# Expert weights in tiles of 4 MB, a ring of 4 slots in place of 8, and two half tiles loaded while the branch products run

## Chip, cores and metric

One core of one Trainium2 chip. The metric is the device time of one execution in microseconds (us), lower is better.

## What is computed

One layer on 256 tokens of width 1024, in float32: a mixer (three attention branches, gates, output projection) and then a mixture of 32 experts, of which each token uses 4. The part that the change touches is the second:

```python
logits = (xt @ w_router + b_router)
top_v, top_e = lax.top_k(logits, TOP_K)          # 4 of 32 experts
wts = softmax(top_v)
# for each block of tokens of one expert e:
hdn = xblk @ w_mlp1[e] + b_mlp1[e]               # 1024 -> 2048
x_glu = minimum(hdn[:, ::2], 7.0)
x_lin = clip(hdn[:, 1::2], -7.0, 7.0)
act = x_glu * sigmoid(1.702 * x_glu) * (x_lin + 1.0)
y = act @ w_mlp2[e] + b_mlp2[e]                  # 1024 -> 1024
# weighted with wts and added to the token's row of x
```

w_mlp1 is 8 MB per expert (units of 2^20 bytes), w_mlp2 4 MB. The whole of both is read once, 402.65 MB (units of 10^6 bytes).

## The kernel before

**Stages.** The mixer runs first (to about 280 us). Its weights come in 40 units of 1 MB (`UNITS`), four in flight in the `raw` tiles (`MIX_RING`). ScalarE and VectorE split each unit in a high and a low part (`mix_high`, `mix_low`), TensorE multiplies. The last ten units are the branch projections (`br_moba0`, `br_ret0`, `br_mem0`, `br_moba1`, `br_ret1`, `br_mem1`) and the output projection (`out0`, `out1`). Then come the routing and the experts.

**Experts.** An item is one expert with up to 64 token slots. The first 30 items are written out, the rest are a loop on a register; with these inputs there are 32 items, one per expert. Of item j TensorE does, in this order and by a program written out by hand: the up products of j (`up`, L1456, four units u of 2 MB of w_mlp1), the gather of the tokens of j + 1 (L1431), the down products of j - 1 (`down`, L1462, two units v of 2 MB of w_mlp2), the transposes of the scatter matrix (L1477), of the next tokens (L1438) and of the activations of j (`act_transposes`, L1483, four of 128 x 128), the biases of j + 1 (L1444, L1446) and the scatter of j - 1 (L1492). Each product has two column halves: 64 slots by 512 columns go to PSUM partitions 0 to 63 and 64 to 127. In item 3 the late part of the routing and the bias of w_mlp2 (`b2`, L1422) stand between the gather and the down products.

**The last item** is written apart: after its up products come the down products of the item before, with `act_transposes` between their two halves, then its own down products, whose second 2 MB come in pieces of 1, 0.5 and 0.5 MB.

**The ring.** 16 MB of SBUF hold eight slots of 2 MB, 16 KB per partition in one contiguous piece of HBM (2 rows of w_mlp1 or 4 rows of w_mlp2). SyncE issues all loads in the order of `LOADS`: the four up units of item 0, then for each j the four up units of j and the two down units of j - 1. A load into a slot waits until TensorE has used what was in it (`up_used`, `down_used`, L511 and L514). Most slots lie over tiles of the mixer, so each of the first eight loads waits for its own part of the mixer (`mixer_left`):

```python
if slot <= 1:
    sp.wait_ge(unit_used, UNITS_DONE[GI["out0"] - 1])
    sp.wait_ge(silu_done, 2)
elif slot == 2:
    sp.wait_ge(y_done, 4)
elif slot == 3:
    sp.wait_ge(unit_used, N_MIX - 2)
```

**Other queues.** GpSimd issues small loads, among them that of `b_mlp2` (`b2s`, L577), which lies in a tile of the moba branch. ScalarE and VectorE each follow their own hand-written order.

Of the kernel before, what the change touches and what calls it, by code (L numbers as in the profile page):

```python
# [16 lines left out]
F32R = mybir.dt.float32r  # L17
# [3 lines left out]
ACT = mybir.ActivationFunctionType  # L21
AX = mybir.AxisListType

P = 128
# [53 lines left out]
USE = {load: n // SLOTS_N for n, load in enumerate(LOADS)}  # L78
LAST_DOWN = [(len(LOADS) + v) % SLOTS_N for v in range(W2U)]
assert not set(LAST_DOWN) & {SLOT[load] for load in LOADS[-IU:]}  # L80

# [123 lines left out]
def build(nc, a, out):  # L205
    ctx = ExitStack()
    with ctx:
# [10 lines left out]
        raw_pair = [sb(f"raw{i}", [P, 4096]) for i in range(MIX_RING // 2)]  # L218
        raw = [raw_pair[i // 2][:, 2048 * (i % 2):2048 * (i % 2) + 2048] for i in range(MIX_RING)]
        first = ExitStack()  # L220
        mix_hi = [sb(f"mix_hi{i}", [P, 2048], F32R, scope=first) for i in range(MIX_HL)]
        first.close()
        hi_pair = sb("hi_raw", [P, 2 * 2048])
# [44 lines left out]
        rt = sb("rt", [NE, 96])  # L268
        selw = sb("selw", [NE, 2, MAX_ITEMS])
        tabT = sb("tabT", [NE, 2, S])  # L270
        PG = sb("PG", [P, 2, TT, MAX_ITEMS])
        posi, gi = PG[:, 0, :, :], PG[:, 1, :, :]
        posm, G = posi[:, :, 0:NE], gi[:, :, 0:NE]
        bsel = sb("bsel", [64, MAX_ITEMS])
        items = sb("items", [1, MAX_ITEMS + 2], I32)

        mix = ExitStack()
# [14 lines left out]
        mix.close()  # L292

# [11 lines left out]
        b2s = o["moba"][0:NE, :, :].rearrange("p t n -> p (t n)")  # L305
        b1raw = PTs[0:64, :]

        merge_pair = [sb(f"merge_raw{i}", [P, 4096]) for i in range(2)]
        first = ExitStack()
        sb("branch_values", [P, 2048], scope=first)  # L310
        mix_hi.append(sb(f"mix_hi{MIX_HL}", [P, 2048], F32R, scope=first))
        first.close()
        value_pair = sb("value_raw", [P, 4096])
# [4 lines left out]
        gate_pair = sb("gate_raw", [P, 4096])  # L318
        b1s = sb("b1s", [P, FF2], F32R)
        prob_pair = sb("prob_raw", [P, 4096])  # L320
# [4 lines left out]
        ends = sb("b2_and_alibi", [P, 2048 + 1536 - 128 - 3 * 256])  # L325
# [4 lines left out]
        ring = merge_pair + [gate_pair, raw_pair[0], value_pair, raw_pair[1], hi_pair, prob_pair]  # L330
# [12 lines left out]
        ring_in = [sem(f"ring_in{i}") for i in range(SLOTS_N)]  # L343
        x_half = [sem(f"x_half{t}") for t in range(TT)]
# [43 lines left out]
        last_part = [sem(f"last_part{i}") for i in range(2)]  # L388
# [32 lines left out]
        def weight_tile(kind, j, u):  # L421

            if isinstance(j, int):
                load = (kind, j, u)
                return ring[SLOT[load]], ring_in[SLOT[load]], 16 * (USE[load] + 1)
            load = (kind, LOOPED if kind == "up" else LOOPED - 1, u)
            return ring[SLOT[load]], ring_in[SLOT[load]], 16 * j + 16 * (USE[load] + 1 - load[1])

        def last_down_tile(v):
            n = len(LOADS) + v  # L430
            return ring[LAST_DOWN[v]], ring_in[LAST_DOWN[v]], 16 * (n // SLOTS_N + 1)

# [23 lines left out]
        def _(sp):  # L456
            for m, (g, hk) in enumerate(UNITS):
# [20 lines left out]
                if m == 5:  # L478
                    sp.dma_start(memT, a["memT"]).then_inc(memT_in, 16)

            w1, w2 = a["w_mlp1"][0], a["w_mlp2"][0]

            def mixer_left(slot):

                if slot <= 1:
                    sp.wait_ge(unit_used, UNITS_DONE[GI["out0"] - 1])
                    sp.wait_ge(silu_done, 2)
                elif slot == 2:
                    sp.wait_ge(y_done, 4)
                elif slot == 3:  # L490
# [1119 lines left out]
```

## Time and profile before

| | |
|---|---|
| median of 3 runs | 1210.91 us (1210.24 to 1213.89) |
| the profiled execution | 1211.36 us |
| its span, first to last instruction | 1209.5 us |
| mean granted TensorE clock | 0.996 |
| PE busy | 1151.7 us (95%) |
| DVE, ACT, POOL busy | 410.5, 225.6, 8.7 us |
| HBM read | 453.11 MB, 375 GB/s over the span |
| expert loads | 191 of 2 MB, one of 1 MB, two of 0.5 MB |

The page calls TensorE's matmuls PE and its weight loads PEld; DVE is VectorE, ACT ScalarE, POOL GpSimd, SP SyncE and SPq its queue of DMA issues. A plain f32 product is recorded as two MATMULs, a transpose as one. "DMA share" is the mean busy share of the 16 DMA engines; it can read slightly over 1. "us to landing" counts from the issue of a DMA to its completion. Times of rows are from the start of the span.

### The profile page before, as it was taken

Reading aid. Unit: us, or ns where it says so; the run is one execution under the profiler, and the core shown is the slowest. Engines: PE = TensorE matmul, PEld = TensorE weight load, DVE = VectorE, ACT = ScalarE, POOL = GpSimd, SP = SyncE. Lnnn points to the kernel's source line nnn. Section 1 sums busy time; section 2 is a strip of 40 time slices with the busy share of each in tenths; the row PEclk is TensorE's granted clock in tenths of the full one; section 3 lists DMA queues with packets and bytes.
Section 4 is the critical chain, followed back from the end, with each engine's and each line's share of the span. In section 5 each row is a group of like instructions: output and inputs, shape, how many; then the busy total and the mean of one; then the engine's idle time right before and its main releaser. Section 6 shows DMA issues by size and latency. Waiting matters only on the chain.

```text
span 1209.5 us, 13242 instructions
## 1 busy us (share of the span) xinstructions
PE 1151.7 (95%) x5401; PEld 536.6 (44%) x5401; DVE 410.5 (34%) x677; ACT 225.6 (19%) x344; POOL 8.7 (1%) x17
## 2 busy tenths in 40 slices
PE   8999999999999999999999999998999999899997
PEld 5888888874333333333433333333333333333332
DVE  4865656864222222222222222222222222222221
ACT  3544447441000000010100000000000000000001
POOL 0100000000000000000000000000000000000000
PEclk9999999999998999999999999999999999999999
DMA  9755454599999999999999999999999999999995
GB/s 352 255 181 169 157 171 157 183 374 429 427 426 423 413 427 429 426 430 424 430 427 429 427 428 428 427 428 429 427 429 427 427 428 430 426 429 426 429 428 237
DMA packets 52322, 454.93 MB, mean 376 GB/s; under 512 B 4368, under 2 KB 4400, under 8 KB 27504
## 3 DMA queue, kind: packets, MB, share of 16 engines
q1 hardware_dynamic: 50816, 449.69, 89.8%
q0 software_dynamic: 784, 2.38, 0.5%
q10 hardware_dynamic: 672, 2.10, 0.5%
q8 instruction: 43, 0.70, 0.2%
q14 instruction: 7, 0.06, 0.0%
HBM read 453.11 MB, written 1.05 MB: 375 GB/s over the span
## 4 chain that ended last, share of the span: by engine, by line
PE 58%; DMA 40%; DVE 1%; issue 1%; ACT 0%; SPq 0%; DVEq 0%; ACTq 0%
PE PS L1456 19%; DMA merge_raw<-in_w_mlp 14%; DMA prob_raw<-in_w_mlp 14%; DMA raw<-in_w_mlp 12%; PE PS L1462 9%; PE PS L1273 6%; PE PS L1275 5%; PE PS L1274 5%; PE PS L1492 3%; PE PS L1431 2%; PE PS L1290 1%; PE PS L1269 1%; PE PS L1438 1%; PE PS L1344 1%; PE PS L1444 1%
## 5 line engine op out<-in xcount | busy, mean ns | idle before, releaser
L1456 PE MATMUL PS<-raw,XG 128*64 128x512 f32 x544 | 123.0, 594 | 11.2 <-DMA raw<-in_w_mlp 11.2
L1185 DVE TENSOR_SCALAR hT<-PS 128x512 f32<-128x512 f32 x32 | 22.1, 692 | 317.7 <-PE PS L1456 317.7
L779 ACT ACTIVATE hT<-hT 128x512 f32<-128x512 f32 x31 | 19.5, 630 | 553.0 <-DVE hT L1185 553.0
L1456 PE MATMUL PS<-merge_raw,XG 128*64 128x512 f32 x480 | 107.5, 596 | 6.2 <-DMA merge_raw<-in_w_mlp 5.9
L857 DVE TENSOR_TENSOR rest<-raw,mix_hi 128x2048 fp32r<-128x2048 f32 x38 | 87.0, 2291 | 55.2 <-ACT mix_hi L631 55.2
L1116 DVE COPY XG<-PS 128x512 f32<-128x512 f32 x32 | 22.1, 692 | 229.0 <-PE PS L1438 229.0
L1123 DVE TENSOR_TENSOR X<-X,PS 128x512 f32<-128x512 f32 x120 | 74.4, 682 | 53.1 <-PE PS L1492 53.1
L1273 PE MATMUL PS<-mix_hi,hTh 128*128 128x512 f32 x224 | 89.8, 401 | 0.0
L1275 PE MATMUL PS<-mix_hi,hTl 128*128 128x512 f32 x224 | 88.2, 394 | 0.0
L1274 PE MATMUL PS<-rest,hTh 128*128 128x512 f32 x224 | 88.1, 393 | 0.0
L631 ACT ACTIVATE mix_hi<-raw 128x2048 fp32r<-128x2048 f32 x38 | 72.6, 1913 | 42.9 <-PE PS L1275 39.9
L1456 PEld LDWEIGHTS PS<-raw,XG 128*64 128x64 f32 x544 | 38.2, 137 | 91.8 <-issue 72.7
L1456 PEld LDWEIGHTS PS<-merge_raw,XG 128*64 128x64 f32 x480 | 32.8, 137 | 77.7 <-issue 62.3
L1456 PE MATMUL PS<-gate_raw,XG 128*64 128x512 f32 x272 | 61.9, 597 | 2.1 <-DMA gate_raw<-in_w_mlp 2.1
L1462 PE MATMUL PS<-merge_raw,AT 128*64 128x512 f32 x256 | 57.4, 594 | 4.9 <-DMA merge_raw<-in_w_mlp 4.9
L1456 PE MATMUL PS<-value_raw,XG 128*64 128x512 f32 x272 | 62.0, 597 | 0.1
L765 ACT ACTIVATE Y<-PS 128x512 f32<-128x512 f32 x31 | 18.6, 599 | 225.4 <-PE PS L1462 225.4
L1431 PE MATMUL PS<-hx,SG 128*64 128x512 f32 x256 | 60.4, 593 | 0.0
L1456 PE MATMUL PS<-prob_raw,XG 128*64 128x512 f32 x240 | 54.3, 594 | 6.2 <-DMA prob_raw<-in_w_mlp 6.2
L1492 PE MATMUL PS<-Y,ST 64*128 64x512 f32 x240 | 59.6, 615 | 0.0
L1462 PE MATMUL PS<-raw,AT 128*64 128x512 f32 x224 | 50.9, 596 | 8.9 <-DMA raw<-in_w_mlp 8.9
L1456 PE MATMUL PS<-hi_raw,XG 128*64 128x512 f32 x240 | 54.6, 597 | 0.0
(272 smaller groups left out, 1246.8 us busy)
## 6 DMA issues: line engine op xcount, KB each, us to landing
raw<-in_w_mlp SPq DMA_DIRECT2D x48, 2048.0 KB, 34.1
merge_raw<-in_w_mlp SPq DMA_DIRECT2D x47, 2048.0 KB, 33.8
gate_raw<-in_w_mlp SPq DMA_DIRECT2D x24, 2048.0 KB, 32.5
value_raw<-in_w_mlp SPq DMA_DIRECT2D x24, 2048.0 KB, 32.7
hi_raw<-in_w_mlp SPq DMA_DIRECT2D x24, 2048.0 KB, 32.3
prob_raw<-in_w_mlp SPq DMA_DIRECT2D x24, 2048.0 KB, 33.8
raw<-in_w_in SPq DMA_DIRECT2D x24, 1024.0 KB, 5.1
raw<-in_w_mem_kv SPq DMA_DIRECT2D x4, 1024.0 KB, 5.1
```

The costliest lines, as they stand in the source:

```text
L631: act.activation(mix_high_part(m)[:, :], raw[m % MIX_RING][:, :], ACT.Copy).then_inc(wh_done, 1)
L857: dve.tensor_tensor(rest[m % MIX_RING][:, :], raw[m % MIX_RING][:, :], mix_high_part(m)[:, :].bitcast(F32), ALU.subtract)\
L1116: dve.tensor_copy(XG[:, :, :].rearrange("p (h c) s -> p h c s", h=2), banks[4].rearrange("p (c h s) -> p h c s", h=2, s=SL)).then_inc(xg, 1)
L1123: dve.tensor_tensor(X[:, t, 512 * n:512 * n + 512], X[:, t, 512 * n:512 * n + 512], scatter_bank(t, n), ALU.add)\
L1185: dve.tensor_scalar(glu, PS[:, 0:1024:2], LIMIT, None, ALU.min).then_inc(swi, 1)
L1273: pe.matmul(pair[gi_ % 2][:, t, :], parts[0][:, k, rows], wh, start=(k == 0), stop=False)
L1274: pe.matmul(pair[gi_ % 2][:, t, :], parts[0][:, k, rows], wl, start=False, stop=False)
L1275: mm = pe.matmul(pair[gi_ % 2][:, t, :], parts[1][:, k, rows], wh, start=False, stop=(k == kc - 1))
L1431: mm = pe.matmul(banks[3][n * SL:(n + 1) * SL, :], SG[:, t, :], hx[:, t, n * 512:(n + 1) * 512], start=(t == 0), stop=(t == 1))
L1456: mm = pe.matmul(PS[h * SL:(h + 1) * SL, n * 512:(n + 1) * 512], XG[:, 2 * u + c, :], tile[:, cols], start=False, stop=(u == W1U - 1 and c ...
L1462: mm = pe.matmul(out[n * SL:(n + 1) * SL, :], parts[:, 4 * v + c, :], tile[:, c * D + n * 512:c * D + (n + 1) * 512], start=(v == 0 and c ...
L1492: pe.matmul(scatter_bank(t, n), ST[rows, t * P:(t + 1) * P], Y[rows, :], start=True, stop=True).then_inc(sc_pe, 1)
```

## The change

- **Tiles.** The eight slots of 2 MB become four of 4 MB. One tile of w_mlp1 is 512 rows, four rows or 32 KB per partition; one tile of w_mlp2 is the expert's whole matrix, eight rows or 32 KB per partition. From the ninth tile on each is one DMA, issued when both halves of the old tile in the slot are used. The first eight tiles come as two halves of 16 KB per partition, each with a semaphore of its own (`half_in`).
- **Order of the first halves.** The second halves of tiles 2 and 3 are issued from within SyncE's list of mixer loads: one after unit 34's load and a wait for the transposes of the memory branch's output, the other after unit 38's load. The other six follow behind the mixer's loads in the order (0,0), (0,1), (1,0), (1,1), (2,0), (3,0).
- **The last down tile** comes in pieces of 2, 1, 0.5 and 0.5 MB in one slot, as before in two.
- **Layouts.** Token rows go to partitions four at a time (`R[:, c:512:4]`), and activations eight at a time. The latter makes 16 products of 64 x 64 with the identity (a step of 8 in the weights) out of four transposes; the copy of their result is then contiguous.
- **SBUF.** `PG`, `rt`, `selw` and `b2s` move into the tile `ends`, the mixer's `mix_hi` tiles to another place. GpSimd's load of `b2s` moves behind its waits for `silu_done` and `y_done`.

```diff
-LOADS = [("up", 0, u) for u in range(W1U)]
+W1T, W2T = W1U // 2, W2U // 2
+IT = W1T + W2T
+LOADS = [("up", 0, u) for u in range(W1T)]
 for _j in range(1, LOOPED + 1):
-    LOADS += [("up", _j, u) for u in range(W1U)] + [("down", _j - 1, v) for v in range(W2U)]
-SLOTS_N = 8
+    LOADS += [("up", _j, u) for u in range(W1T)] + [("down", _j - 1, v) for v in range(W2T)]
+SLOTS_N = 4
+IN_HALVES = 8
...
-        ring = merge_pair + [gate_pair, raw_pair[0], value_pair, raw_pair[1], hi_pair, prob_pair]
+        ring = [merge_tile, raw_tile, prob_tile, head_tile]
...
+            def up_half(n, h):
+
+                kind, j, t = LOADS[n]
+                rows = w1[j, 512 * t:512 * t + 512, :].rearrange("(p k) n -> p k n", k=4)
+                sp.dma_start(ring[n % SLOTS_N][:, 4096 * h:4096 * h + 4096].rearrange("p (k n) -> p k n", k=2), rows[:, 2 * h:2 * h + 2, :])\
+                    .then_inc(half_in[n % SLOTS_N][h], 16)
...
+            def up_tile(e, t, tile, landed):
+                sp.dma_start(tile[:, :], w1[e, 512 * t:512 * t + 512, :].rearrange("e (p k) n -> p (e k n)", k=4)).then_inc(landed, 16)
+
+            def down_tile(e, tile, landed):
+                sp.dma_start(tile[:, :], w2[e, :, :].rearrange("e (p k) n -> p (e k n)", k=8)).then_inc(landed, 16)
+
+            def used(n, h=1):
+
+                kind, j, t = LOADS[n]
+                if kind == "up":
+                    sp.wait_ge(up_used, W1U * j + 2 * t + h + 1)
+                else:
+                    sp.wait_ge(down_used, W2U * j + h + 1)
...
+                if m == UNITS_DONE[GI["br_moba0"]] + MIX_RING - 1:
+                    sp.wait_ge(task_done, TASKS[("oT", "mem", TT - 1)] + 1)
+                    up_half(2, 1)
+                if m == UNITS_DONE[GI["br_ret1"]] + MIX_RING - 1:
+                    sp.wait_ge(unit_used, UNITS_DONE[GI["br_ret1"]])
+                    up_half(3, 1)
+
+            sp.wait_ge(unit_used, UNITS_DONE[GI["br_mem1"]])
+            sp.wait_ge(silu_done, 2)
+            up_half(0, 0)
+            sp.wait_ge(y_done, 4)
+            sp.wait_ge(unit_used, max(m for m in SPLIT_UNITS if HI_SLOT[SPLIT_UNITS.index(m)] == MIX_HL) + 1)
+            up_half(0, 1)
+            sp.wait_ge(unit_used, N_MIX - 2)
+            up_half(1, 0)
+            sp.wait_ge(unit_used, N_MIX)
+            up_half(1, 1)
+            sp.wait_ge(b1l, 1)
+            up_half(2, 0)
+            up_half(3, 0)
+            for n in range(SLOTS_N, IN_HALVES):
+                for h in range(2):
+                    used(n - SLOTS_N, h)
+                    if LOADS[n][0] == "up":
+                        up_half(n, h)
+                    else:
+                        down_half(n, h)
+            for n in range(IN_HALVES, len(LOADS) - IT):
+                kind, j, t = LOADS[n]
+                used(n - SLOTS_N)
+                if kind == "up":
+                    up_tile(slice(j, j + 1), t, ring[n % SLOTS_N], ring_in[n % SLOTS_N])
...
-            pool.dma_start(b2s, a["b_mlp2"][0]).then_inc(b2_in, 16)
             pool.dma_start(bsel[:, 0:NE], a["misc"][0:64, 4 * P + 64:4 * P + 64 + NE]).then_inc(b2_in, 16)
             pool.memset(b1s[64:P, :].bitcast(F32), 0.0).then_inc(zeroed, 1)
             pool.wait_ge(silu_done, 2)
             pool.wait_ge(y_done, 4)
+            pool.dma_start(b2s, a["b_mlp2"][0]).then_inc(b2_in, 16)
...
-                for c in range(4):
-                    mm = pe.transpose(out[:, c * P:(c + 1) * P], act_t[:, c:512:4], ident)
+                for c in range(KC):
+                    for h in range(2):
+                        rows = slice(h * SL, (h + 1) * SL)
+                        mm = pe.matmul(out[rows, c * SL:(c + 1) * SL], act_t[:, c:512:KC], ident[:, rows], start=True, stop=True)
                 mm.then_inc(tr_pe, 1)
```

## Rows read from the trace of the kernel before

**Rows 1.** The page: busy us (share of the span) and instructions of each engine.
```profile
PE 1151.7 (95%) x5401; PEld 536.6 (44%) x5401; DVE 410.5 (34%) x677; ACT 225.6 (19%) x344; POOL 8.7 (1%) x17
```

**Rows 2.** Windows: stretch, length, busy time of each engine, PEclk, DMA share, GB/s.
```profile
327.00:606.00 279.00, 278.17 (x1294) 103.53 (x1292) 74.92 (x151) 26.98 (x50) 0.00 (x0) 0.98 1.01 425
...
700.00:900.00 200.00, 183.32 (x852) 65.19 (x850) 45.91 (x90) 18.91 (x35) 0.00 (x0) 1.00 1.01 428
```

**Rows 3.** The chain that ended last, in order: start us, us, what.
```profile
419.49 13.88 PE PS L1456 x64
...
442.80 0.49 PE PS L1483 x4
...
446.13 13.88 PE PS L1456 x64
...
693.76 7.04 PE PS L1456 x32
...
1047.95 7.04 PE PS L1456 x32
```

**Rows 4.** Timeline of SyncE's queue (SPq), 240 to 420 us: start us, us, DMA.
```profile
245.61 0.92 SPq L511 DMA_DIRECT2D merge_raw<-in_w_mlp  x2
247.65 0.33 SPq L511 DMA_DIRECT2D gate_raw<-in_w_mlp  x1
257.24 0.33 SPq L511 DMA_DIRECT2D raw<-in_w_mlp  x1
...
369.07 0.33 SPq L514 DMA_DIRECT2D raw<-in_w_mlp  x1
385.26 0.33 SPq L511 DMA_DIRECT2D value_raw<-in_w_mlp  x1
...
396.46 0.33 SPq L511 DMA_DIRECT2D hi_raw<-in_w_mlp  x1
399.90 0.33 SPq L511 DMA_DIRECT2D prob_raw<-in_w_mlp  x1
```

**Rows 5.** By source line: landing of the loads of 369.07, 396.46 and 399.90.
```profile
DMA to landing us min/median/max: 19.7/19.7/19.7
...
DMA to landing us min/median/max: 8.8/8.8/8.8
...
DMA to landing us min/median/max: 10.3/10.3/10.3
```

**Rows 6.** The chain that ended last, behind the issue of the last load.
```profile
1164.11 29.02 DMA merge_raw<-in_w_mlp
```

**Rows 7.** Timeline of TensorE, last item: start us, us, line, operation.
```profile
1166.68 3.65 PE L1456 MATMUL PS<-gate_raw,XG 128*64 128x512 f32 x16
...
1183.57 3.65 PE L1462 MATMUL PS<-hi_raw,AT 128*64 128x512 f32 x16
1187.15 0.75 PE L1483 MATMUL PS<-misc,hT 128*128 128x128 f32 x4
1188.28 3.65 PE L1462 MATMUL PS<-prob_raw,AT 128*64 128x512 f32 x16 [0.39 <-DMA prob_raw<-in_w_mlp]
```

**Rows 8.** Timeline of TensorE's weight loads near 371 us: start us, us, line.
```profile
370.68 0.29 PEld L1414 LDWEIGHTS PS<-selw,tabT 32*128 32x128 f32 x2 [0.81 <-issue]
...
372.11 0.19 PEld L1417 LDWEIGHTS PS<-selw,misc 32*64 32x64 f32 x2
```

**Rows 9.** Lines by form, weight loads of transposes: busy us, mean ns.
```profile
L1483 PEld LDWEIGHTS PS<-misc,hT 128*128 128x128 f32 x128 | 18.4, 211 | 0.8 <-issue 0.8
...
L1290 PEld LDWEIGHTS PS<-misc,hx 128*128 128x128 f32 x56 | 6.4, 145 | 0.6 <-issue 0.3
```

**Rows 10.** Queue q1 in 120:180, 700:900, 1193.5:1195.5: packets, MB, share of 16 engines.
```profile
q1 hardware_dynamic: 4338, 8.59, 44.0%
...
q1 hardware_dynamic: 5864, 85.45, 100.4%
...
q1 hardware_dynamic: 90, 0.41, 50.0%
```

More of the change, by code:

```diff
@@ L217, in build @@
         first.close()
[L218 to L223, printed above, removed]
+        raw_tile = sb("raw", [P, 8192])
+        raw = [raw_tile[:, 2048 * i:2048 * i + 2048] for i in range(MIX_RING)]
         X = sb("X", [P, TT, D])
@@ L343, in build @@
         ring_in = [sem(f"ring_in{i}") for i in range(SLOTS_N)]
+        half_in = [[sem(f"half_in{i}_{h}") for h in range(2)] for i in range(SLOTS_N)]
         x_half = [sem(f"x_half{t}") for t in range(TT)]
@@ L387, in build @@
         sc_pe, sc_add = sem("sc_pe"), sem("sc_add")
-        last_part = [sem(f"last_part{i}") for i in range(2)]
+        last_part = [sem(f"last_part{i}") for i in range(4)]
         end_act, end_dve = sem("end_act"), sem("end_dve")
@@ L479, in _ @@
                     sp.dma_start(memT, a["memT"]).then_inc(memT_in, 16)
[L481 to L490, printed above, removed]
-                    sp.wait_ge(unit_used, N_MIX - 2)
-                elif slot == 4:
-                    sp.wait_ge(y_done, 4)
-                    sp.wait_ge(unit_used, max(m for m in SPLIT_UNITS if HI_SLOT[SPLIT_UNITS.index(m)] == MIX_HL) + 1)
-                else:
-                    sp.wait_ge(unit_used, N_MIX)
-                    sp.wait_ge(b1l, 1)
@@ L528, in load_item @@
                 e = expert(j)
-                for u in range(W1U):
-                    sp.wait_ge(up_used, W1U * (j - 1) + u + 1)
-                    tile, landed, _ = weight_tile("up", j, u)
-                    load_w1(e, u, tile, landed)
+                for t in range(W1T):
+                    sp.wait_ge(up_used, W1U * (j - 1) + 2 * t + 2)
+                    slot = SLOT["up", LOOPED, t]
+                    up_tile(e, t, ring[slot], ring_in[slot])
                 e = expert(j - 1)
-                for v in range(W2U):
-                    sp.wait_ge(down_used, W2U * (j - 2) + v + 1)
-                    tile, landed, _ = weight_tile("down", j - 1, v)
-                    load_w2(e, v, tile, landed)
+                sp.wait_ge(down_used, W2U * (j - 2) + 2)
+                slot = SLOT["down", LOOPED - 1, 0]
+                down_tile(e, ring[slot], ring_in[slot])
             late_in_sbuf(sp, ("tab",))
@@ L1449, in up @@
             def up(j, u):
-                tile, landed, count = weight_tile("up", j, u)
+                tile, landed, count = weight_half("up", j, u)
                 pe.wait_ge(landed, count)
@@ L1467, in down @@
             def down(j, v):
-                tile, landed, count = weight_tile("down", j, v)
+                tile, landed, count = weight_half("down", j, v)
                 pe.wait_ge(landed, count)
@@ L1561, in _ @@
             for v in range(W2U):
-                tile, landed, count = last_down_tile(v)
+                tile = last_down_half(v)
                 if v == 1:
@@ L1568, in _ @@
                         pe.matmul(banks[LAST_BANK[t, n]], STL[rows, t * P:(t + 1) * P], Y[rows, :], start=(n == 1), stop=False)
[L1569 removed]
                 for c in range(4):
[L1571 to L1572 removed]
+                    if 4 * v + c in (0, 4, 6, 7):
+                        pe.wait_ge(last_part[(0, 4, 6, 7).index(4 * v + c)], 16)
                     mm = down_products(tile, AT2, banks[0], v, c)
```

105 lines of the change are left out of this document (43 added, 62 removed).

## The prediction, made before the change was run

> **What bounds the kernel now.** The order of reading is: the page's busy line, the windows by stretch, the chain of waits, SyncE's queue. The busy line gives TensorE 95% [rows 1], which looks like the bound. The windows correct this: from 327 us on the DMA engines have no free time either (share 1.01, 425 to 428 GB/s) [rows 2]. The chain says which of the two ends last, and where it changes. Early on the expert stage is TensorE's own pace: an item's up products begin at 419.49 and the next item's at 446.13, 26.64 us apart [rows 3]. Later the chain alternates with landings, and twelve items take 693.76 to 1047.95, 29.52 us each [rows 3]. So DMA is the slower server, and a full ring of 16 MB hides that for some ten items. The end is therefore the time at which the DMA engines last ran dry, plus the bytes left by the pace, plus what TensorE does behind the last landings.
>
> When do they last run dry? SyncE issues a load at 369.07 and the next only at 385.26, because the ring is full [rows 4]; the first lands 19.7 us after its issue, at 388.8 [rows 5]. The load of 396.46 lands after 8.8 us, at 405.3 [rows 5]: one 2 MB load takes 4.92 us in the stream (below), so it found an empty queue and 3.9 us are issue and completion. The next, 399.90, lands 10.3 us later at 410.2, right behind it [rows 4, 5]. From there nothing is late until the last down product: its first 2 MB land at 1193.13 [rows 6]. Between 405.26 and 1193.13 lie 160 loads (the 31st of 192 to the 191st): 787.87 / 160 = **4.924 us per 2 MB**.
>
> **The change part by part.** The sum is made against the profiled execution, 1211.36 us (span 1209.5), which is 0.45 above the median of the runs, 1210.91.
>
> *Two halves begun in the branches.* They would start while the branch and output weights are loaded, before 245.61, instead of behind the mixer's last product. One other half starts later: up_half(0, 1) now waits for the same units as the load of 257.24, where three 2 MB loads were out by 247.65 [rows 4]. Whatever is won before 385 is lost again, since the ring is full there and the restart is set by TensorE's use of a slot. I cost the head start at nothing; its cover is that full ring, and without it it would be worth at most its two loads, 9.8 us. The mixer's own loads are issued four units ahead, so 4.9 us more in their queue is hidden; SyncE's new wait for the memory branch's transposes holds only mixer loads that would wait for their own units anyway. The bias load that moves behind y_done on GpSimd's queue starts near 247.65, since one of SyncE's loads had the same wait [rows 4]; the first gather matrix waits for it, after the whole output projection and the routing, and only a memset stands behind it.
>
> *Coarser restart, 3.3 us lost.* A 4 MB slot is free when both halves are used. The two 2 MB loads of 396.46 and 399.90 become one 4 MB load issued at 399.90. On an empty queue it lands after 3.9 + 9.75 = 13.65 us, at 413.5, where the second of the old ones landed at 410.2.
>
> *The activation transposes, d per item.* The 8-row layout of w_mlp2 needs blocks of 64 x 64, so four transposes become 16 plain f32 products. A plain f32 product is recorded twice (an item's 32 up products are the x64 of [rows 3]), so 32 weight loads of 64 columns replace 4 of 128. The four cost 0.49 us [rows 3]. No row shows the new shape. Two plain f32 loads of 128 columns take 0.29 us and two of 64 columns 0.19 us [rows 8]: 0.05 us for each 64 columns. That is the low end, 32 x 0.05 - 0.49 = 1.1 us (below it only if neighbouring products on the two column halves overlap, say 0.5). The columns are also read with a step of 8: transposed loads with a step take 211 ns against 145 without [rows 9], 33 ns per 64 columns; whether a plain load pays this is open. With all of it 0.083 us each, d = 2.2; by the old transposes' 0.12 us each, d = 3.4, the high end. I take half of the step's price, 0.066 us, near the nearest row: **d = 1.6 us**. It lies on TensorE's own order, so the use that restarts the stream at 399.90 comes 4d = 6.4 us later (items 0 to 3). After that it is hidden, 26.64 + 1.6 against a DMA pace of 3 x 9.75 = 29.2, until the end.
>
> The Trainium skill, in "SBUF — State Buffer", section "Door 1: The DMA port swizzle", says that reads which cross to a new 16-byte line each time pay a penalty, so f32 may be strided up to 4 elements. The rows do show a dearer strided load (211 against 145 ns), but already the step of 4. By that rule each of the new reads pays in full, d = 2.2 instead of 1.6, and the time is that of the second rival below, 1225 against 1217.5.
>
> *The tail, 3.0 + d lost.* Now down of the last item but one comes as two loads. Its first half runs from 1183.57, the transposes from 1187.15, its second half from 1188.28, on landing [rows 7]. As one load all 4 MB land with the old second half. Then 3.58 + 0.74 + 3.65 = 7.97 us and d stand before the last down product, whose weights land 4.92 later: 3.0 + 1.6 = 4.6 us more. The pieces of the very last load are cut as before.
>
> *The pace, 7.9 us won.* From 700 to 900 us, 85.45 MB take 100.4% of 16 x 200 us, 37.6 ns per KB of 1000 bytes; in the tail, in 4 KB pieces, 16 us for 0.41 MB, 39.0; in the mixer, in 2 KB pieces, 422 us (44.0% of 16 x 60) for 8.59 MB, 49.2 [rows 10]. A fixed cost x per piece explains the first pair with 8 ns (1.4 over 1/4.1 - 1/16.4) and the outer pair with 27 ns (11.6 over 1/2.05 - 1/16.4). The mixer's loads stand alone and their first pieces wait, so I take **12 ns**, near the low end. A 4 MB load has 16 pieces of 16 KB on each engine, or 8 of 32 KB: 0.1 us saved. 79 such loads lie between the restart and the last but one down: 7.9 us (bounds 5 and 17). No row has a piece over 16 KB; if they are cut again, nothing is won.
>
> Sum: 3.3 + 6.4 + 4.6 - 7.9 = **+6.4 us**, 1217.8 against the profiled execution, 1217.4 against the median. I say 1217.5.
>
> **The rivals.**
> 1. *The new products run side by side.* d = 0.5: 3.3 + 2.0 + 3.5 - 7.9 = +0.9, **1212**. For it: products on the two column halves overlap in the up stage (64 recorded ones in 13.88 us, 0.217 each [rows 3]). Against: here the weight loads are the longer part.
> 2. *TensorE becomes the bound* (slower). Without waits item 31 begins at 446.13 + 25 x 26.64 + 31d = 1112.1 + 31d, and reaches the last down product 24.9 + d later (1183.57 - 1166.68 [rows 7], then 7.97 + d): 1137 + 32d. The DMA chain has it there at 1193.13 + 3.3 + 3.0 - 7.9 + 5d. They cross at d = 2.0. With the full price of the step, d = 2.2, it is +14, **1225**; with 0.1 us each, 1241.
> 3. *The pieces are not 32 KB on the engines* (the change doesn't do what it says): +14.3, **1225.5**. Nothing in the trace speaks for or against.
> 4. *The fixed cost is that of the mixer's row*, 27 ns: 17.1 us won, and with d between 0.5 and 1.1, -5 to -8: **1204.5**. For it: the row; against it: the 4 KB row.
> 5. *Longer strides in HBM cost rate*: neighbouring partitions now read 32 KB apart. No row shows any loss; each percent costs 7.9 us, with the 12 ns gone about **1233**. The Trainium skill, "DMA: Bandwidth & Descriptors", section "Latency and other measured facts", reports such losses for row pitches that are large powers of two, from 512 KiB; no run here shows that.
>
> **How the numbers follow.** Forecast 0.36, rival 1 0.15, rival 2 0.18, rival 3 0.08, rival 4 0.20, rival 5 0.03. 0.3% (3.6 us) is about what a measurement of this kernel can tell from no change. Slower: nearly all of the forecast (0.31), rivals 2, 3 and 5: 0.60. Same: rival 1 mostly, rests of the forecast and rival 4: 0.22. Faster: rival 4, 0.18. The range 1205.5 to 1227 leaves out part of rivals 4 and 2, and rival 5.
>
> **What would show it.** Right: the transposes' line near 2.1 us per item; the restart load landing near 420 us instead of 410; 4 MB every 9.75 us between landings; the last down product starting right behind the one before, without a wait for DMA. Wrong: a pace of 9.85 (rival 3) or 9.6 (rival 4); an item pace over 29.2 us with no waits for DMA (rival 2); the ring not full near 385, which would make the head start count.

## The result and the profile after

| | kernel before | kernel after |
|---|---|---|
| median | 1210.83 us (4 runs, 1210.24 to 1213.89) | 1223.24 us (4 runs, 1221.75 to 1224.13) |
| ratio, 95% interval | 1 | 1.0096 (1.0075 to 1.0117) |
| profiled execution, its span | 1211.36, 1209.5 | 1224.13, 1222.1 |
| TensorE busy | 1151.7 us | 1204.0 us |

The change costs about 1%. The forecast, 1217.5, had the sign; its sum of +6.4 us was half of the 12.6 us between the two spans. The page of after, busy us and instructions of each engine, then the main DMA queue:

```profile
PE 1204.0 (99%) x6297; PEld 596.5 (49%) x6297; DVE 410.2 (34%) x677; ACT 225.6 (18%) x344; POOL 8.7 (1%) x17
...
q1 hardware_dynamic: 38288, 449.68, 88.4%
```

Against [rows 1] TensorE has 896 more recorded weight loads and as many more products. The queue moves its 449.68 MB in 38288 packets; in 700 to 900 us there are 2953 for 85.95 MB, where [rows 10] has 5864 for 85.45. Of the 2953 packets 330 are under 512 bytes; the other 2623 hold 32 KB each. So the engines do move 32 KB at once, and rival 3 is out.

SyncE's queue around the restart, the load of 409.02 that is issued when the DMA engines have run dry (start us, us), then by source line the time from issue to landing of the loads of 409.02, 415.89, 424.47 and 437.45, all in after:

```profile
396.03 0.33 SPq L478 DMA_DIRECT2D prob_raw<-in_w_mlp  x1
409.02 0.33 SPq L478 DMA_DIRECT2D head_raw<-in_w_mlp  x1
415.89 0.33 SPq L481 DMA_DIRECT2D merge_raw<-in_w_mlp  x1
424.47 0.33 SPq L478 DMA_DIRECT2D raw<-in_w_mlp  x1
```
```profile
DMA to landing us min/median/max: 12.2/12.2/12.2
...
DMA to landing us min/median/max: 16.5/16.5/16.5
...
DMA to landing us min/median/max: 17.7/17.7/17.7
...
DMA to landing us min/median/max: 15.8/15.8/15.8
```

The restart that stood at 399.90 and landed at 410.2 [rows 4, 5] is now issued at 409.02 and lands at 421.2, 11.0 us later. The next three land at 432.4, 442.2 and 453.3: 11.2, 9.8 and 11.1 us apart. One clean load takes 9.7 (below), so the first and the third gap are 1.4 us too long. Windows of after (stretch, length, busy time by engine, clock, DMA share, GB/s) tell which of this is idle time of the DMA engines:

```profile
327.00:606.00 279.00, 278.17 (x1490) 113.61 (x1488) 71.33 (x145) 25.77 (x48) 0.00 (x0) 0.98 0.97 413
```
```profile
392.00:396.00 4.00, 4.00 (x21) 1.27 (x18) 0.00 (x0) 0.00 (x0) 0.00 (x0) 1.00 0.04 16
408.00:412.00 4.00, 4.00 (x22) 1.39 (x20) 0.00 (x0) 0.00 (x0) 0.00 (x0) 1.00 0.62 188
412.00:439.00 27.00, 27.00 (x150) 10.95 (x148) 7.08 (x14) 2.70 (x5) 0.00 (x0) 1.00 1.01 436
439.00:443.00 4.00, 4.00 (x22) 1.40 (x20) 0.00 (x0) 0.00 (x0) 0.00 (x0) 1.00 0.92 328
```

The stretch that ran at 1.01 and 425 GB/s in [rows 2] is down to 0.97 and 413. The engines are idle ahead of the loads of 396.03 and 409.02, and a third, smaller loss lies at 439 to 443 us, behind the late issue of 437.45: that is the third gap. The first gap is no idle time, for between 412 and 439 us the engines are never short of work. There the landing of the restart load itself came early: it stands 2.5 us over its transfer (12.2 - 9.7), and both loads together 4.0 (432.4 - 409.02 - 2 x 9.7).

From one item in the chain of after (start us, us, what), in which TensorE waits for nothing:

```profile
430.39 13.88 PE PS L1472 x64
...
453.71 2.07 PE PS L1501 x32
...
458.83 6.58 PE PS L1472 x29
```

28.43 us from 430.39 to 458.83, where [rows 3] have 26.64: d is 1.79 us. 1.58 of it is the line of the transposes, 2.07 against 0.49; 0.2 are behind it, in the bias products. Behind the restart the chain first waits for a landing at 844.84, where before it did at 646.65. The end of the same chain:

```profile
1145.22 21.98 DMA head_raw<-in_w_mlp
...
1167.24 7.09 PE PS L1478 x32
...
1197.18 3.58 PE PS L1478 x16
...
1202.62 6.87 PE PS L1478 x32
```

The 6.87 us at 1202.62 are the second down half of the last item but one and the first of the last, 3.44 each. So the last down product begins near 1206.0, where before it began at 1193.27 behind the landing of [rows 6]. The load of the last item but one's down tile is issued at 1174.51 and lands 22.2 us later, at 1196.7; TensorE comes to it at 1197.18 by its own order and doesn't wait.

### The profile page after: what moved, and what is told of

Same layout as the page of the kernel before. It is cut to its first block, busy times and chain, and to the rows that moved or that the text cites. A ratio compares the mean times of both kernels' runs of the same rounds, so it can differ in the third digit from the quotient of the medians.

```text
span 1222.1 us, 14925 instructions
## 1 busy us (share of the span) xinstructions
PE 1204.0 (99%) x6297; PEld 596.5 (49%) x6297; DVE 410.2 (34%) x677; ACT 225.6 (18%) x344; POOL 8.7 (1%) x17
## 3 DMA queue, kind: packets, MB, share of 16 engines
q1 hardware_dynamic: 38288, 449.68, 88.4%
HBM read 453.11 MB, written 1.05 MB: 372 GB/s over the span
## 4 chain that ended last, share of the span: by engine, by line
PE 80%; DMA 18%; DVE 1%; issue 1%; ACT 0%; SPq 0%; DVEq 0%; ACTq 0%
PE PS L1472 28%; PE PS L1478 15%; DMA merge_raw<-in_w_mlp 8%; DMA prob_raw<-in_w_mlp 8%; PE PS L1289 6%; PE PS L1291 6%; PE PS L1290 5%; PE PS L1501 4%; PE PS L1510 4%; PE PS L1447 3%; DMA head_raw<-in_w_mlp 2%; PE PS L1460 1%; PE PS L1285 1%; PE PS L1306 1%; PE PS L1454 1%; PE PS L1462 1%
## 5 line engine op out<-in xcount | busy, mean ns | idle before, releaser
L1472 PE MATMUL PS<-prob_raw,XG 128*64 128x512 f32 x544 | 120.3, 594 | 0.0
L1472 PE MATMUL PS<-raw,XG 128*64 128x512 f32 x544 | 120.1, 594 | 0.0
L1201 DVE TENSOR_SCALAR hT<-PS 128x512 f32<-128x512 f32 x32 | 22.1, 692 | 286.1 <-PE PS L1472 286.1
L1472 PE MATMUL PS<-head_raw,XG 128*64 128x512 f32 x480 | 105.9, 594 | 0.0
L1132 DVE COPY XG<-PS 128x512 f32<-128x512 f32 x32 | 22.1, 691 | 217.0 <-PE PS L1454 217.0
L1472 PEld LDWEIGHTS PS<-prob_raw,XG 128*64 128x64 f32 x544 | 38.2, 137 | 79.1 <-issue 78.3
L1501 PE MATMUL PS<-misc,hT 128*64 128x64 f32 x1024 | 68.4, 286 | 0.0
L1472 PEld LDWEIGHTS PS<-head_raw,XG 128*64 128x64 f32 x480 | 33.9, 137 | 69.8 <-issue 68.7
L1501 PEld LDWEIGHTS PS<-misc,hT 128*64 128x64 f32 x1024 | 64.3, 216 | 4.2 <-issue 0.5
L1478 PE MATMUL PS<-head_raw,AT 128*64 128x512 f32 x288 | 63.7, 593 | 1.6 <-DMA head_raw<-in_w_mlp 1.6
## 6 DMA issues: line engine op xcount, KB each, us to landing
prob_raw<-in_w_mlp SPq DMA_DIRECT2D x4, 2048.0 KB, 10.7
```

Source lines behind the costliest of these rows:

```text
L1132: dve.tensor_copy(XG[:, :, :].rearrange("p (h c) s -> p h c s", h=2), banks[4].rearrange("p (c h s) -> p h c s", h=2, s=SL)).then_inc(xg, 1)
L1472: mm = pe.matmul(PS[h * SL:(h + 1) * SL, n * 512:(n + 1) * 512], XG[:, 2 * u + c, :], tile[:, cols], start=False, stop=(u == W1U - 1 and c ...
L1478: mm = pe.matmul(out[n * SL:(n + 1) * SL, :], parts[:, 4 * v + c, :], tile[:, c * D + n * 512:c * D + (n + 1) * 512], start=(v == 0 and c ...
L1501: mm = pe.matmul(out[rows, c * SL:(c + 1) * SL], act_t[:, c:512:KC], ident[:, rows], start=True, stop=True)
```

## The experiments

The kernels named a_, c_ and g_ are the kernel after with one edit, b_ is the kernel before with one edit, and d_ and e_ take something from both. The kernel before was run beside each group, with medians of 1210.62 to 1210.84 us.

**The transposes back, and the transposes alone.**

The edit of a_four_transposes, in act_transposes; b_sixteen_products has the same edit the other way round, in the kernel before:

```diff
-                for c in range(KC):
-                    for h in range(2):
-                        rows = slice(h * SL, (h + 1) * SL)
-                        mm = pe.matmul(out[rows, c * SL:(c + 1) * SL], act_t[:, c:512:KC], ident[:, rows], start=True, stop=True)
+                for c in range(4):
+                    mm = pe.transpose(out[:, c * P:(c + 1) * P], act_t[:, c:512:4], ident)
```

In both kernels the order of the transposed activations no longer fits that of the down weights' rows, so the down products multiply other pairs, as many as before.

> The changed kernel with the four 128 x 128 activation transposes of before in place of the 16 products; the activations then lie in the wrong order for w_mlp2 (this part of the computation is changed), the work is otherwise the same. Theory (the extra 1.79 us per item delay the load that restarts the full ring, four times over, and the tail once): 1223.2 - 7.2 - 1.8 = 1214 us, the restart load issued near 402 instead of 409.02. Rival (TensorE's extra work is hidden behind DMA, the loss is the 4 MB granularity alone): only the tail gives way, 1221.5 us or more.

> The kernel before with the 16 products in place of the four transposes and nothing else; the activations then lie in the wrong order (this part of the computation is changed). Theory (the part of the change that costs most is this one, and it acts through the restart of the full ring): 4 x 1.79 = 7.2 us more, 1218; the last item hides it, since its second half is late anyway. Rival (hidden behind DMA, which is the bound): 1211.

Measured: a_four_transposes 1211.55 us, ratio to before 1.0004 (0.9994 to 1.0013); b_sixteen_products 1217.80, ratio 1.0053 (1.0037 to 1.007). The 16 products cost 11.7 us in the kernel after and 7.0 in the kernel before. With the four transposes, SyncE's restart is back where it was before:

```profile
400.28 0.33 SPq L478 DMA_DIRECT2D head_raw<-in_w_mlp  x1
```

400.28 stands for 409.02: 8.7 us, where four items' d are 7.2. The other 1.5 us are not the products' own. In item 3, behind the small products of the late routing, the granted clock falls to the lower of its two levels (1.2 of 2.4 GHz; 0.50 from 375 to 383 us in before) for a while, and in a_four_transposes for a shorter one. Windows of TensorE in before and in a_four_transposes (stretch, length, busy, clock, DMA share, GB/s):

```profile
372.00:392.00 20.00, 19.17 (x66) 0.74 1.01 423
```
```profile
372.00:392.00 20.00, 19.17 (x78) 0.83 0.91 378
```

From the routing's first small product to the next item's up products that is 22.1 us in before and 20.6 here, with the same work (in the chains, 370.75 to 392.84 and 372.65 to 393.23); in after it is 23.9, one d more than in before. So 7.2 of the 8.7 us are the products' own. b_sixteen_products, which has the clock of before there (0.74), has its restart at 407.21 for 399.90, 7.3 us later. The end of the chain of a_four_transposes:

```profile
1163.81 21.82 DMA head_raw<-in_w_mlp
...
1185.67 3.65 PE PS L1478 x16
```

Here the last item but one's down tile is waited for, to 1185.63, as the prediction had it. With 16 products the end of the chain has no such wait, neither in after nor in b_sixteen_products.

**Where on TensorE's order time costs anything.**

The edit of c_sixteen_late, in act_transposes; the branch that is left out holds the 16 products as they were:

```diff
+                if isinstance(j, int) and j < 8:
+                    for c in range(4):
+                        mm = pe.transpose(out[:, c * P:(c + 1) * P], act_t[:, c:512:4], ident)
+                else:
...
```

> The kernel after, with four 128x128 transposes in items 0 to 7 and the 16 products from item 8 on (where the four stand, the activations come out in another order than the down weights need, so that part of the products is computed with the wrong rows; the amount of work is the same). Theory: TensorE's time counts only before the last time the DMA engines run dry (items 0 to 3) and behind the last landing. The restart then stands as with four transposes throughout (loads issued at 400 and 407 us), and of the 11.7 us between that kernel (1211.55) and the kernel after (1223.24) only the tail's 1.4 to 1.8 us come back: 1213. Rival: time added on TensorE counts in every item, because TensorE has become the bound: 24 of 32 items, 1211.5 + 0.75 x 11.7 = 1220.3.

Measured 1213.73 us, ratio 1.0028 (1.0017 to 1.0039). The 16 products in 24 of 32 items cost 2.2 us over a_four_transposes, and the eight early ones 9.5. SyncE's restart stands at 399.84; item 3 had the shorter stretch at the lower clock here too, so some 1.5 of the 9.5 us are the clock's. Which of the eight items count was not tried. So time added on TensorE behind the last dry queue is hidden until the tail, as the prediction has it; the rival's 1220.3 is out.

**What the 16 products are made of.**

In g_strides act_transposes chooses by j % 7. The forms 0 to 6 stand here in order (loops and indents left out); in form 6 the loop over the halves h goes around the loop over c:

```diff
+ pe.matmul(out[rows, c * SL:(c + 1) * SL], act_t[:, c:512:8], ident[:, rows], start=True, stop=True)
+ pe.matmul(out[rows, c * SL:(c + 1) * SL], act_t[:, first:first + 253:4], ident[:, rows], start=True, stop=True)
+ pe.matmul(out[rows, c * SL:(c + 1) * SL], act_t[:, first:first + 127:2], ident[:, rows], start=True, stop=True)
+ pe.matmul(out[rows, c * SL:(c + 1) * SL], act_t[:, 64 * c:64 * c + 64], ident[:, rows], start=True, stop=True)
+ pe.transpose(out[:, c * P:(c + 1) * P], act_t[:, c:512:4], ident)
+ pe.transpose(out[:, c * P:(c + 1) * P], act_t[:, c * P:(c + 1) * P], ident)
+ pe.matmul(out[rows, c * SL:(c + 1) * SL], act_t[:, c:512:8], ident[:, rows], start=True, stop=True)
```

> The kernel after, where the activation transposes change their form from item to item in turns of seven (only the first and the last form take the right columns to the right places for the down weights; in the others that part of the products is computed from the wrong rows, with the same amount of work). Each form has a line of its own, so the profile gives its busy time per item: 16 products of 64 columns read with a step of 8 (2.07 us so far), of 4, of 2 and of 1; four transposes of 128 columns with a step of 4 (0.48) and of 1; and the 16 of step 8 with the two column halves not in turns but one half after the other. Theory of the forecast: a fixed part near 0.05 us per weight load, 1.5 us for the 32 at step 1, and a surcharge that is whole from step 4 on: 2.07 at step 4, 1.8 at step 2. Rival 1: the step costs nothing on such short loads, the number of loads alone counts: 2.07 in all four. Rival 2: only steps above 4 elements pay: 1.5 at steps 1, 2 and 4. Rival 3: products on the two column halves overlap; without turns 2.07 becomes 2.5 or more.

Groups of instructions by line, TensorE's products, then its weight loads (count | busy us, mean ns of one). L1503 is form 0, L1508, L1513 and L1518 are forms 1 to 3, L1529 is form 6. An item has 32 of them, so L1503 stands for 7 items, L1508 for 5 and the others for 4:

```profile
L1503 PE MATMUL PS<-misc,hT 128*64 128x64 f32 x224 | 14.9, 285 | 0.0
L1529 PE MATMUL PS<-misc,hT 128*64 128x64 f32 x128 | 14.5, 286 | 0.0
L1508 PE MATMUL PS<-misc,hT 128*64 128x64 f32 x160 | 10.7, 286 | 0.0
L1513 PE MATMUL PS<-misc,hT 128*64 128x64 f32 x128 | 4.7, 226 | 0.0
L1518 PE MATMUL PS<-misc,hT 128*64 128x64 f32 x128 | 4.6, 225 | 0.0
```
```profile
L1503 PEld LDWEIGHTS PS<-misc,hT 128*64 128x64 f32 x224 | 14.1, 216 | 1.2 <-issue 0.5
...
L1508 PEld LDWEIGHTS PS<-misc,hT 128*64 128x64 f32 x160 | 10.0, 215 | 0.6
L1513 PEld LDWEIGHTS PS<-misc,hT 128*64 128x64 f32 x128 | 4.2, 138 | 0.5
```

The kernel was run once (1218.31 us), and only its lines are read. Busy time per item: 2.1 us at step 8 (14.9 / 7), 2.1 at step 4 (10.7 / 5), 1.2 at step 2 and at step 1 (4.7 / 4, 4.6 / 4), 3.6 at step 8 with one column half after the other (14.5 / 4); the four transposes of 128 columns have 0.65 at step 4 and 0.6 at step 1. Three things follow. The surcharge for a step is all or nothing: none at 2, whole at 4 and 8. It comes to 0.031 us a load (2.13 - 1.15 over 32); the fixed part is 0.036. And products on the two column halves do overlap: out of turns they cost 0.113 each, in turns 0.067. The theory held at steps 4 and 8; it was too dear at step 1 (1.5 us for 1.2) and missed step 2 (1.8 for 1.2). Rivals 1 and 2 are out, rival 3 held.

**The head start.**

```diff
                 if m == UNITS_DONE[GI["br_moba0"]] + MIX_RING - 1:
                     sp.wait_ge(task_done, TASKS[("oT", "mem", TT - 1)] + 1)
-                    up_half(2, 1)
...
-                    up_half(3, 1)
...
             up_half(2, 0)
+            up_half(2, 1)
             up_half(3, 0)
+            up_half(3, 1)
```

> The changed kernel with the two halves of the branch stage issued last, behind the mixer's last unit, like the other halves. Theory (whatever the head start wins is lost in the full ring before 410 us): the same time within 1 us, 1223. Rival 1 (the head start is worth its two loads): 9.8 us more, 1233. Rival 2 (the two halves slow the mixer, whose first expert tile is used 2.0 us later than before, 288.1 against 286.1): that use goes back to 286.1 and the time to 1221.

Measured 1223.32 us, ratio 1.01 (1.0084 to 1.0117), against 1223.24 of after. Its restart is at 408.32 for 409.02. Windows of after and of this kernel, TensorE, clock, DMA share, GB/s:

```profile
300.00:350.00 50.00, 49.30 (x276) 1.00 0.95 396
...
385.00:425.00 40.00, 39.17 (x193) 0.92 0.81 334
```
```profile
300.00:350.00 50.00, 49.30 (x274) 1.00 1.01 429
...
385.00:425.00 40.00, 39.17 (x201) 0.94 0.89 370
```

What the early halves give is given back as idle DMA engines from 286 to 425 us: the full ring takes it, as predicted.

**The size of the pieces.**

The edit in up_tile; down_tile is cut in the same way, with h=2 and k=4:

```diff
-                sp.dma_start(tile[:, :], w1[e, 512 * t:512 * t + 512, :].rearrange("e (p k) n -> p (e k n)", k=4)).then_inc(landed, 16)
+                sp.dma_start(tile[:, :].rearrange("p (h x) -> p h x", h=2), w1[e, 512 * t:512 * t + 512, :].rearrange("e (h p k) n -> p (e h) (k n)", h=2, k=2)).then_inc(landed, 16)
```

> The changed kernel with each 4 MB load cut into two pieces of 16 KB per partition, 2 MB apart in HBM; the rows then meet the wrong rows of the activations (this part of the computation is changed), bytes and counts are the same. Theory (9 to 10 ns of fixed cost per piece): 4 MB take 9.79 us instead of 9.71, over some 80 tiles 6 us more, 1229. Rival 1 (the length of the pieces doesn't matter): 1223. Rival 2 (27 ns per piece, as the mixer's row suggested): 17 us more, 1240.

Measured 1229.00 us, ratio 1.0147 (1.013 to 1.0164): 5.8 over after. Six loads of 4 MB lie between the ends of two waits in either chain, first after, then this kernel:

```profile
871.95 31.18 DMA merge_raw<-in_w_mlp
...
930.24 31.18 DMA prob_raw<-in_w_mlp
```
```profile
873.19 32.05 DMA merge_raw<-in_w_mlp
932.35 31.62 DMA prob_raw<-in_w_mlp
```

(961.42 - 903.13) / 6 = 9.715 us and (963.97 - 905.24) / 6 = 9.788: 0.073 us for eight pieces fewer on each engine, 9 ns a piece. The loads of 2 MB in 16 KB pieces, whose landings in before stand 4.89 us apart where nothing disturbs them, give the same 9.78 for 4 MB; so it is the length of the pieces and not where they lie in HBM.

**The restart in finer loads, and the tail in finer loads.**

The one edit of c_fine_restart, and that of c_tail_halves in load_item (indexes of the rows cut):

```diff
-IN_HALVES = 8
+IN_HALVES = 20
...
-                sp.wait_ge(down_used, W2U * (j - 2) + 2)
-                down_tile(e, ring[slot], ring_in[slot])
+                for h in range(2):
+                    sp.wait_ge(down_used, W2U * (j - 2) + h + 1)
+                    sp.dma_start(ring[slot][:, 4096 * h:4096 * h + 4096]..., w2[e]...[:, 4 * h:4 * h + 4, :]).then_inc(half_in[slot][h], 16)
```

> The kernel after, with the first 20 loads of the ring, not 8, cut into two halves of 2 MB, each waiting for its own half of the slot. Theory: at the restart one 4 MB load costs 1.8 us against two of 2 MB, and the two loads behind it, which found the queue nearly empty, 1.4 us each; 12 more loads in 16 KB pieces cost 0.08 us each. 4.6 less 1.0: 1219.6. Rival: the size of the first loads is hidden by TensorE's pace until 800 us, and nothing comes back: 1223 to 1224.

> The kernel after, with the down tiles of the last three items but one (those whose loads stand in the loop over the items) loaded as two DMAs of 2 MB, each waited for by itself. Theory: the first half of the last item but one's down products then runs while its second half lands, 2.9 us earlier, for 0.2 us of smaller pieces: 1220.5. Rival: TensorE itself has no free time at the end and the last landing is not what it waits for: 1223.2.

Measured: c_fine_restart 1222.16 us, ratio 1.0095 (1.0079 to 1.011); c_tail_halves 1222.80, ratio 1.0095 (1.0079 to 1.011). Neither is told apart from after, and both miss what was expected, 3.6 and 2.7 us less. For the restart a part is in the trace: at the landing of the tile of 452.14 its stream is 5.4 us ahead of that of after (467.31 for 472.69; 0.8 of it since its first expert tile is released at 287.33 for 288.12), but the whole loads that follow are issued late again (465.12 lands 10.8 us behind the one ahead), and at 518.59 for 521.24 only 2.7 are left. The rest stays open: in the profiled executions the last wait ends 2.9 us earlier than in after (1142.55 + 21.76 = 1164.31 for 1167.20), the medians show 1.1, and single executions of after alone have spans from 1219.8 to 1222.2. For the tail the chain of c_tail_halves is plain:

```profile
1106.41 31.19 DMA merge_raw<-in_w_mlp
...
1137.74 7.09 PE PS L1488 x32
...
1166.40 6.87 PE PS L1488 x32
```

The wait that ended at 1167.20 is gone, and TensorE comes to the same product at 1166.40, 0.8 us earlier, because everything from 1137.74 on is its own work. At the end the kernel after is bound by both servers within a microsecond, so a finer tile there is worth 0.4 us by the medians and not 3.

**A version of both.**

d_blocks_fine is the kernel after with IN_HALVES = 20, with the four transposes and the activation copies of the kernel before, and with each down tile as two loads of 512 rows (the line of down_half below). e_fine_ends adds two loads for each up tile in load_item. e_no_head_start is e_fine_ends with the edit of a_no_head_start.

```diff
-                rows = w2[j].rearrange("(p k) n -> p k n", k=8)
+                rows = w2[j, 512 * h:512 * h + 512, :].rearrange("(p k) n -> p k n", k=4)
...
+                    for h in range(2):
+                        sp.wait_ge(up_used, W1U * (j - 1) + 2 * t + h + 1)
...
```

> A version meant to keep the good of both: up tiles as one piece of 32 KB per partition, down tiles in two blocks of 512 rows (two loads of 2 MB in 16 KB pieces, the rows as in the kernel before), so that four 128x128 transposes serve; the first 20 loads in halves. From the kernel after with four transposes, 1211.5: the tail's 2.9 and the restart's 1.8 come back, 26 down tiles in smaller pieces cost 2.1 and 8 more up tiles 0.6: 1209.5, and 1208 if loads behind the restart no longer find an empty queue. Before is at 1210.8, so faster by 1 to 3 us. Rival: nothing of restart and tail comes back, 1213 to 1214.

> As d_blocks_fine, but the up tiles of the last two items (whose loads stand in the loop over the items) also come as two loads of 2 MB each. In the trace of d_blocks_fine TensorE waits last for the second 4 MB up tile of the last item, to 1175.05, and does all the rest without a wait. Theory: with the halves it begins that tile's first half 4.9 us earlier and waits last for the down halves, 2.0 us earlier at the end, for 0.3 us of smaller pieces: 1.7 below d_blocks_fine, 1209.7, and 1 to 2 us below before. Rival: as with the down tiles of the kernel after, TensorE's own order takes the wait's place and nothing moves: 1211.4.

> e_fine_ends without the early start: the second halves of the third and fourth slot are loaded behind the others, and not while the branch products run. Theory: the ring is full before 386 us in any case, so nothing changes: the same as e_fine_ends within 0.5 us. Rival: where the DMA engines no longer run dry at the restart (0.5 us of gap in d_blocks_fine against 6 in the kernel after), two loads begun early are 4 MB less to load behind it: 5 to 9.8 us slower than e_fine_ends.

Measured: d_blocks_fine 1211.39 us, ratio 1.0003 (0.9994 to 1.0012), no better than before where 1 to 3 us less were expected; e_fine_ends **1209.09**, ratio 0.9987 (0.9978 to 0.9996), 1.5 us faster than before and the fastest here; e_no_head_start **1217.94**, ratio 1.0052 (1.0038 to 1.0066). The chain of d_blocks_fine has its last wait at a 4 MB up tile:

```profile
1153.25 21.80 DMA prob_raw<-in_w_mlp
```

Behind it TensorE waits for nothing more. With the up tiles in halves the last wait is for the last down tile again, as in [rows 6]; of e_fine_ends:

```profile
1161.58 29.23 DMA merge_raw<-in_w_mlp
...
1190.95 3.65 PE PS L1486 x16
```

The head start makes 8.9 us between these two and nothing in after. The end of the chain of e_no_head_start:

```profile
1168.65 29.41 DMA merge_raw<-in_w_mlp
...
1198.19 5.28 PE PS L1482 x16
```

The first 2 MB of the last down tile land at 1198.06 for 1190.81: 7.3 us is what the head start is worth. The other 1.6 are in the product behind it, 5.28 us for 3.65: behind the wait for it the clock stood at the lower level for a while (0.79 in the mean of 1196 to 1204 us, 1.00 in e_fine_ends). The loads of the same line between 396 and 401 us, from issue to landing, first e_fine_ends, then e_no_head_start:

```profile
DMA to landing us min/median/max: 8.4/9.2/9.9
```
```profile
DMA to landing us min/median/max: 13.6/13.6/13.6
```

The first of e_fine_ends takes 8.4 us, close to the 8.8 of [rows 5], where a little time was lost: with the head start the DMA engines are just about to run dry there. 13.6 is about one 2 MB load more in the queue: without the head start they never run dry at the restart, and every byte that was not loaded early is loaded at the end. Two loads are 9.8 us; of these e_fine_ends gives some back earlier, at 286 to 292 us, where its engines have a share of 0.71 (254 GB/s) and those of e_no_head_start 0.99 (423 GB/s), about 2.4 us. My theory for e_no_head_start (the ring is full before 386 us in any case) was wrong: in the new ring several slots come free later than in the old one. Its first loads, as after issues them:

```profile
218.28 0.34 SPq L468 DMA_DIRECT2D prob_raw<-in_w_mlp  x1
240.96 0.50 SPq L468 DMA_DIRECT2D head_raw<-in_w_mlp  x1
247.47 12.03 SPq L468 DMA_DIRECT2D merge_raw<-in_w_mlp  x2
259.55 11.94 SPq L468 DMA_DIRECT2D raw<-in_w_mlp  x2
```

At 250 us three loads are out in after, as in the kernel before [rows 4], but only because two of them are the early ones; without them it is one. The head start mainly pays for what the new order of slots holds back.

## Why the prediction was right, and where it was wrong

The restart's landing and the stream up to the last item but one's down tile, from the rows above, beside the terms of the sum:

| step | predicted | measured |
|---|---|---|
| head start | 0 | 0 (0.1 between the medians) |
| mixer, first expert tile used | not named | +2.0 |
| four items' transposes before the restart | +6.4 | +7.2 (4 x 1.79) |
| restart in one 4 MB load | +3.3 | +3.2 (1.8 at its landing, 1.4 at the next) |
| a second, short stall at 439 to 443 us | not named | +1.4 |
| pace of the stream | -7.9 | -5.4 |
| tail | +4.6 | +4.2 |
| sum | +6.4 | +12.6 |

1. *Head start: right, for the reason given.* The step also said what it is worth without its cover, at most 9.8 us; where the cover is gone the last tile lands 7.3 us earlier with it. That the cover is the restart itself, so that whoever mends the restart uncovers the head start, I had not drawn from it.

2. *The transposes' place: right.* Only the items before the last dry queue and the tail pay. c_sixteen_late and a_four_transposes show it: 9.5 us from the first eight items (some 1.5 of it the clock's), 2.2 from the other 24.

3. *Their price: 1.6 for 1.79, from two errors that cancel.* The prediction built a load from 0.05 us and half of a surcharge of 0.033. The runs have 0.036 and the whole of 0.031. The half was the step that failed: the row of the 211 ns transposes [rows 9] already was the whole price, and a plain load of 64 columns pays it too. That the base was too dear because the two 64-column loads of [rows 8] have no second column half to overlap with is likely, but was tried at step 8 only; rival 1's mechanism is real, in turns 0.067 and out of turns 0.113, and without it d would have been above 3. By the rule of the Trainium skill, "SBUF — State Buffer", section "Door 1: The DMA port swizzle", two reads in each 16-byte line give full speed and every read that comes to a new line pays. Weight loads at steps 4 and 8 take 215 and 216 ns and at step 2, with two reads in each line, 138, so the trace agrees with that. The same note of the Trainium skill lets f32 be strided by up to 4 elements for free; the trace does not, for step 4 pays in full, and the measurement decides.

4. *The restart: its term held, and one was missing.* The load of 409.02 landed after 12.2 us, 2.5 beside the transfer of 9.7 and not the 3.9 of the prediction, but the next load brought the rest: two transfers and 4.0 us from 409.02 to 432.4, with no idle time of the engines between 412 and 439 us. Why the first landing is early stays open; the load of 396.03, on an empty queue as well, took 13.6 us, 3.9 over its transfer. What the prediction read from [rows 5] was not right, though its number serves: the load of 396.46 did not find an empty queue. The one ahead of it, of 388.69, landed 10.4 us after its issue, at 399.1, and the two landings are 6.2 us apart where a transfer takes 4.9: 1.3 us were lost there. Missing was the stall of 1.4 us behind it. The prediction let the stream run at its own pace from the restart load on, as it had in the kernel before. But a slot of 4 MB comes free every 6.9 to 13 us (SyncE's rows), and a transfer takes 9.7: the load of 437.45 was issued 13.0 us after the one before it, and only 4.7 before that one landed. a_four_transposes got back 11.7 us, 2.7 more than five times d; 1.5 of that is item 3's clock, and in its trace this stall is missing, since its load of 426.93 comes 6.2 us before the landing ahead of it (433.14, next 442.85). The stall is the coarser ring's own price beside the restart's, and I had counted the two as a single event.

5. *The pace: -7.9 that was -5.4.* The mechanism holds, the size was a choice of 12 ns a piece between ends of 8 and 27 (eight pieces and 79 loads of it are 7.6 us, the 7.9 came by rounding to 0.1 a load); it is 9. The nearest row was right: the 8 ns of the 4 KB pieces, not the single loads of the mixer. Rival 4 is out.

6. *The tail: right in size, wrong in kind.* 4.2 us for 4.6, but not because one load replaces two; halving that load gave back 0.4. TensorE arrives 0.5 us behind the landing by itself. This is the second rival's mechanism, TensorE as the bound, confined to the last two items: the crossing point of 2.0 us was worked out for the whole stage and d is 1.79, so TensorE is 0.7 us per item faster than the DMA engines, and the last items' extra products (two of 1.05 us and one of 0.59, L1567 and L1571 in the chain) are more than that. That they alone use it up was not tried.

7. *The mixer: not named.* The first expert tile is released at 288.12 us and was at 286.14. Windows of TensorE from 60 to 120 us, before and after:

```profile
60.00:120.00 60.00, 60.00 (x290) 1.00 0.53 178
```
```profile
60.00:120.00 60.00, 60.00 (x286) 1.00 0.51 172
```

No expert load is under way in that stretch, and a_no_head_start has 286 there too, so it is not the head start. The buffers of the mixer lie at other places in the kernel after; whether that is the cause was not tried and stays open. In after it stands in the restart's time in full, since it comes ahead of it (409.02 - 399.90 is 7.2 + 2.0 within 0.1); what the end would gain without it was not tried either.

The signs of each part were right. The pace (2.5), the mixer (2.0) and the missing stall (1.4) were the largest errors, and all fell on the same side. That the time lies in the stated range is in part luck: the tail's 4.2 us and the transposes' price came out near by other ways than those predicted. What I would now add to such a prediction: when a slot doubles, play the first four or five loads behind a dry queue one by one, not the first alone.

## What to carry to other kernels

Find the moment at which the stream last runs dry: time on the other engine ahead of it costs in full, time behind it is free up to the tail, so a change that lengthens one step in all of 32 items by 1.8 us cost 12 us in one kernel and 7 in the other, not 57, and not 0. A head start is worth its transfer only if the ring never fills behind it; measure that before it is built, and again once the stall behind it is mended. When two kernels differ by one or two microseconds, compare the granted clock of the same stretch first: a lower clock in item 3 or behind the last wait made up 1.5 and 1.6 us here. And larger pieces should not be bought with a dearer layout on the other side: 9 ns for each 16 KB piece was 5.8 us in all, the 16 products that its layout needed were 11.7.

## What the runs showed of the hardware

- TensorE's weight loads of 64 f32 columns: a step of 2 is free (138 ns a recorded load, as at step 1), and a step of 4 or 8 costs 78 ns more of busy time, 31 ns on the path (g_strides).
- Small products with 64 columns at step 8 on alternating column halves take 0.067 us each, on one half after the other 0.113: the order of the loops was worth 1.5 us per item.
- A DMA piece of 32 KB saves 9 ns against two of 16 KB, 0.7% of the transfer; the 4 MB are otherwise moved at the same rate, with neighbouring partitions 32 KB apart in HBM, which shows no loss (430 GB/s in 700 to 900 us for 428 before; rival 5 is out).
- A load of 4 MB issued as the queue had run dry took 12.2 or 13.6 us in after, 2.5 or 3.9 beyond its transfer; one of 2 MB took 7.2 in c_fine_restart (391.82 and 404.82), 2.3 beyond it. Landings can stand 11.2 us apart while the engines are busy throughout, so a late landing alone doesn't show idle engines.
